# A fifth slot for expert weights in the memory of the modulation rows; modulation product on TensorE, state-space quarters begun among the projections

## What is computed

```
ada = silu(c) @ w_ada + b_ada
shift1, scale1, gate1, shift2, scale2, gate2 = split(ada, 6)
u = rms_norm(h, norm1_g) * (1 + scale1) + shift1
u_ssm, q, k, v, q_idx, k_idx, w_idx, g_ssm, g_attn = split(u @ w_in)
y_ssm = s5_mixer(u_ssm, ...)                     # diagonal complex scan, 32 groups x 64 states, GLU
y_attn = dsa_attention(q, k, v, q_idx, k_idx, w_idx)   # index scores, top-k keys, 8 heads, ALiBi
mixed = sigmoid(g_ssm) * (y_ssm @ w_proj_ssm) + sigmoid(g_attn) * (y_attn @ w_proj_attn)
h = h + gate1 * (mixed @ w_out)
u2 = rms_norm(h, norm2_g) * (1 + scale2) + shift2
h = h + gate2 * moe_ffn(u2)                      # sigmoid router, 64 experts of width 256, one shared
out = rms_norm(h, norm_f_g)
```

## Time and profile before

| | |
|---|---|
| Time, median of three runs | 1305.91 us (1305.76 to 1308.87) |
| Profiled execution | 1307.59 us, its span 1305.8 us |
| PE busy | 1139.6 us, 87% |
| DVE, ACT, POOL busy | 558.1, 221.6, 253.8 us |
| Issue to landing, median: w_ada piece, w_in item | 12.1 us, 9.1 us (2 MB each) |
| Issue to landing, median: expert gate, up, down | 11.8, 17.1, 17.5 us (1 MB each) |
| Bytes moved by DMA | 318.47 MB |

### The profile page before, as it was taken

One profiled execution on the slowest core, in us unless ns is written; L12 is line 12 of the kernel. 1 busy time (PEld: TensorE's weight loads), 2 busy tenths in 40 slices (PEclk: granted clock), 3 DMA queues, 4 the chain that ended last, 5 costly groups with the idle time before them and its releaser, 6 DMA issues. The chain is left out here.

```text
span 1305.8 us, 14750 instructions
## 1 busy us (share of the span) xinstructions
PE 1139.6 (87%) x5464; PEld 542.3 (42%) x5465; DVE 558.1 (43%) x1157; ACT 221.6 (17%) x440; POOL 253.8 (19%) x244
## 2 busy tenths in 40 slices
PE   0799677897999999998798999999999999998854
PEld 0544455644455444443433343444334344343222
DVE  5325989977745311334452222322222222222138
ACT  2411231104233200012001111111111111111101
POOL 7852477200000000002001111111111111111000
PEclk9799788898889999998998999999999999998977
DMA  8725100143131412120679999999999999999676
GB/s 326 187 94 180 55 10 10 42 161 129 35 159 64 162 64 81 65 88 18 241 290 348 422 404 416 417 408 419 416 389 416 398 421 387 403 399 396 245 323 265
DMA packets 84044, 318.47 MB, mean 244 GB/s; under 512 B 28978, under 2 KB 32050, under 8 KB 55298
## 3 DMA queue, kind: packets, MB, share of 16 engines
q1 hardware_dynamic: 64084, 277.96, 53.8%
q0 software_dynamic: 13488, 36.23, 7.2%
q10 hardware_dynamic: 6400, 3.33, 1.2%
HBM read 300.57 MB, written 28.31 MB: 252 GB/s over the span
## 5 line engine op out<-in xcount | busy, mean ns | idle before, releaser
L1526 PE MATMUL ps<-uTs,ring 128*128 128x512 f32 (+2 forms) x496 | 228.6, 619 | 3.4 <-DMA ring<-in_w_in 2.7
L1827 PE MATMUL ps<-ring,XT 128*32 128x512 f32 (+1 forms) x1472 | 216.7, 603 | 9.9 <-DMA ring<-in_w_exp_up 8.7
L1526 PEld LDWEIGHTS ps<-uTs,ring 128*128 128x128 f32 (+2 forms) x496 | 95.7, 197 | 123.0 <-issue 118.4
L1388 DVE TENSOR_TENSOR uTs<-uTs,ps 128x256 f32<-128x256 f32 x44 | 18.5, 421 | 281.3 <-ACT uTs L1007 281.3
L743 POOL DMA_INDIRECT XT<-u_rows,idx x45 | 45.9, 1020 | 400.9 <-DVE idx L1377 383.5
L1827 PEld LDWEIGHTS ps<-ring,XT 128*32 128x32 f32 (+1 forms) x1472 | 66.0, 120 | 137.9 <-issue 133.7
L1857 PE MATMUL ps<-ring,uTs 128*32 128x512 f32 (+1 forms) x736 | 112.5, 614 | 0.7 <-DMA ring<-in_w_exp_down 0.6
L1794 PE MATMUL ps<-ring,XT 128*128 128x512 f32 x224 | 98.4, 592 | 0.0
L1429 DVE TENSOR_SCALAR uTs<-ps,gat 128x512 f32<-128x512 f32 x44 | 33.1, 751 | 120.9 <-PE ps L1857 80.4
L596 POOL TENSOR_TENSOR ring<-ring 128x512 f32<-128x512 f32 (+4 forms) x35 | 56.8, 1622 | 79.3 <-issue 28.0
L1074 DVE SCALAR_TENSOR_TENSOR ADA<-ring,sm,ADA 128x2048 f32<-128x2048 f32 x24 | 60.2, 2507 | 27.5 <-DMA ring<-in_w_ada 13.9
(11 more groups left out here) (319 smaller groups left out, 1363.4 us busy)
## 6 DMA issues: line engine op xcount, KB each, us to landing
ring<-in_w_exp_gate SPq DMA_DIRECT2D x64, 1024.0 KB, 11.8
ring<-in_w_exp_up SPq DMA_DIRECT2D x64, 1024.0 KB, 17.1
ring<-in_w_exp_down SPq DMA_DIRECT2D x64, 1024.0 KB, 17.5
ring<-in_w_ada SPq DMA_DIRECT2D x12, 2048.0 KB, 12.1
ring<-in_w_in SPq DMA_DIRECT2D x7, 2048.0 KB, 9.1
ring<-expert_rows SPq DMA_DIRECT2D x6, 2048.0 KB, 18.4
ring<-in_w_out SPq DMA_DIRECT2D x2, 2048.0 KB, 8.7
H<-in_x SPq DMA_DIRECT2D x1, 2048.0 KB, 13.9
```

The costliest lines, as they stand in the source:

```text
L1526: ins = mm(b[0:rows_, 0:cols], l, r, start=(k == 0), stop=(k == len(chunks) - 1))
L1827: ins = mm(a3(ps[0][c, :], 2), xgT[par][:, k, c], wgu[r][:, k], start=(k == 0), stop=(k == KD - 1))
```

## The change

The products of silu(c) with w_ada move from DVE to PE. A piece is eight products: a column of silu(c) repeated 32 times as the stationary side, 512 weight columns moving, and four quarters of the 2048 columns in four 32-row parts of one PSUM bank, which is kept for it (`NB` falls from 6 to 5). DVE adds the bias once for each group of four pieces (`ada_row`), and `ada` picks a row with a column of the identity. The modulation rows no longer need 6144 columns of all partitions for long, so `ADA` becomes the fifth expert slot (`SLOTS`); the last modulation row moves to `GATE2`, the small table K16s into `ADA`. x is loaded first. The chunks of u are loaded before ("gs", 0). The first quarter's build and chunks are placed among the qi projections, its application before all index scores, and the build of the next quarter between gs and y. DVE's `top_k` of the second block moves into the first block's heads, that of the third into the second block's. POOL makes tables 2 and 3 earlier by a place.

```diff
-NB = 6
+NB = 5
 RING = 4
+SLOTS = RING + 1
...
+            sp.dma_start(H[:], a["x"][0].rearrange("(t p) d -> p t d", p=P)).then_inc(S["x_in"], 16)
...
             load(("A", 0))
-            sp.dma_start(H[:], a["x"][0].rearrange("(t p) d -> p t d", p=P)).then_inc(S["x_in"], 16)
             load(("A", 1))
...
             sp.dma_start(wg[3], weights("w_exp_gate", e3)).then_inc(gu_in[3], 16)
+            done(sp, ("gP", 0))
+            load_gate_up(4, e4)
+            load_down(4, e4)
             done(sp, ("dn", TT - 1, 1))
             sp.dma_start(wu[3], weights("w_exp_up", e3)).then_inc(gu_in[3], 16)
...
             s5_tables(1)
+            s5_tables(2)
             causal(1)
+            s5_tables(3)
             causal(2)
-            s5_tables(2)
             causal(3)
-            s5_tables(3)
...
+            def ada_row(part):
+
+                dve.wait_ge(b_in[part], 64)
+                dve.wait_ge(S["ada_sum"], 4 * (part + 1))
+                V.tensor_tensor(ada_rows[part], ada_rows[part], ps[5][:, :], ALU.add).then_inc(S["ada_row"], 1)
...
+            for q in range(NQ):
+                s5_scan(q)
+                if q + 1 < NQ:
+                    s5_phases(q + 1)
+                    s5_kernel(q + 1)
+                    index_scores(q + 1)
+            top_k(1, 0, 16)
+            ada_row(1)
...
-                    if n < TOPK // 8:
-                        top_k(3, n, n + 1)
+                    if i < 2:
+                        top_k(2 + i, 2 * h, 2 * h + 2)
...
+            def ada_piece(n):
+
+                part, j = n // 4, n % 4
+                w = a3(arrived(pe, ("A", n)), 2)
+                if n == 0:
+                    pe.wait_ge(S["c_silu"], 1)
+                elif j == 0:
+                    pe.wait_ge(S["ada_row"], part)
+                for k in range(2):
+                    col = csil[:, 2 * j + k:2 * j + k + 1].broadcast_to((P, 32))
+                    for q in range(4):
+                        ins = mm(ps[5][32 * q:32 * (q + 1), :], col, w[:, k, 512 * q:512 * (q + 1)],
+                                 start=(j == 0 and k == 0), stop=(j == 3 and k == 1))
+                ins.then_inc(S["ada_sum"], 1)
...
-            for c in range(2 * KD):
-                ins = mm(b[:, c:c + 1], ADA[:, P * c:P * (c + 1)], ones[:, 0:1], start=True, stop=True)
+            for c in range(4):
+                ins = tr(b[:, P * c:P * (c + 1)], ada_rows[0][:, P * c:P * (c + 1)])
...
+            ada_piece(4)
             s5_apply(0)
-            s5_build(1)
-            indexer(3)
-            s5_apply(1)
-            s5_build(2)
-            s5_apply(2)
-            s5_build(3)
-            s5_apply(3)
+            taken(pe, ("qiT", 3))
+            for q in range(1, NQ):
+                indexer(q)
+                s5_apply(q)
             w = a3(arrived(pe, ("q", 0)), 8)
             for m in range(4):
                 projection_t("qT", m, w, P * m)
+            ada_piece(7)
```

More of the change, by code:

```diff
@@ L504, in _ @@
                 load_down(n, e)
-            e2, e3 = expert_id(2), expert_id(3)
+            e2, e3, e4 = (expert_id(n) for n in range(2, 5))
             done(sp, ("out", TT - 1, 1))
@@ L538, in _ @@
                 with sp.If(n_ov > u):
-                    sp.wait_ge(S["expert_done"], LAST_PASS[NE - RING + u] + 1)
+                    sp.wait_ge(S["expert_done"], LAST_PASS[max(n for n in range(NE) if n % SLOTS == u)] + 1)
                     further(u, u)
@@ L1092, in rms_scale @@
                 link(V.tensor_tensor(rstd[:, c], rstd[:, c], newt[:, c], ALU.mult))
-            for n in range(2):
-                ada_piece(n)
             dve.wait_ge(S["squares"], 1)
@@ L1609, in _ @@
                 transposed_rows("uT", t, ut4)
[L1610 removed]
+            ada_piece(2)
+            ada_piece(3)
+            pe.wait_ge(S["ada_row"], 1)
             b = begin(("mod", 0))
[L1612 to L1613 removed]
+            for c in range(4):
+                ins = tr(b[:, P * c:P * (c + 1)], ada_rows[0][:, P * c:P * (c + 1)])
             end(ins)
[L1615 to L1616 removed]
             w = a3(arrived(pe, ("ssm", 0)), 8)
             for t in range(TT):
[L1619 removed]
+                b = begin(("ssm", t))
+                for k in range(KD):
+                    if t == 0:
+                        pe.wait_ge(S["u_ok_s" if k % 2 else "u_ok_v"], k // 2 + 1)
+                    ins = mm(b[:, :], uT[:, k, P * t:P * (t + 1)], w[:, k], start=(k == 0), stop=(k == KD - 1))
+                end(ins)
             pe.wait_ge(S["ct_in"], 256)
@@ L1633, in _ @@
             w = a3(arrived(pe, ("qi", 0)), 8)
-            for m in range(4):
+            for m in range(2):
                 projection_t("qiT", m, w, P * m)
-            taken(pe, ("qiT", 3))
+            s5_build(0)
+            projection_t("qiT", 2, w, P * 2)
+            chunks(0)
+            projection_t("qiT", 3, w, P * 3)
             def gates(name, half):
```

189 lines of the change are left out of this document (83 added, 106 removed).

## The result

The changed kernel takes 1298.1 us (median of 7 runs, 1295.9 to 1300.5); the kernel before, run beside it, 1310.3. The ratio is **0.9908**, with an interval of 0.9892 to 0.9925: 12 us faster, where 35 were forecast and the range ended at 1288. The forecast was counted from 1305.9; the ratio applied to that gives 1293.9, which is outside the range as well. The profiled execution has a span of 1296.5 us against 1305.8.

What follows compares the result with a forecast made beforehand. Three engines handing work over bound it to 293 us, PE to 640, full DMA engines with PE nearly full from 677. Terms -18 - 16 + 1.8 + 7.5 + 1 - 11 = -34.7 took 1305.9 to 1271 us; range 1256 to 1288.

Steps and rivals of the forecast that it cites:

- Start: Up to the ssm product: x loaded first and no accumulation on DVE, start at 35.5 us against 53.4, -18 us.
- Rival 4: The four 32-column products of a piece run one after another: 6.9 us instead of 1.8, total 1321 us; chance 0.04.
- the changes of tile shape: On PE: 24 changes cost 2.4 us at worst, taken as nothing; a drain of one record each would be 10 us.
- Quarters: Four state-space quarters: ends at 134, 168, 202 and 229 us against 262.8 for the last, -16 us beyond the start's gain.
- Elsewhere five are enough: Five accumulator banks instead of six suffice outside the glu and branch products, as each needed group was emptied earlier.
- First logits: Between the quarters and attention: the modulation piece behind q adds +1.8 us.
- Attention: Four blocks: -1.3 first, +5.3 second, +1.8 each third and fourth, sum +7.5; with about +1 behind it, +8.5.
- the +1.0 forecast: Behind attention, between glu and branch products: five accumulator banks and the bias row cost PE about +1 us.
- The +7.5: The sum of the four attention blocks in us, with bounds 0 and +13.
- Experts: Expert passes: the fifth slot fills the idle DMA gap, everything lands 7.6 us earlier, fewer waits for weights: -11 us.
- the five rivals: Slower tables 1283 (0.2), better slot and attention 1256 to 1264 (0.16), useless slot 1282 (0.09), serial tiles 1321 (0.04), unchanged (0.02).

Runs made afterwards that it cites:

- tables_later: Changed kernel with SyncE waiting for the modulation's fourth piece before issuing the state-space tables: ratio 0.99 to the kernel before.
- short_pieces: Changed kernel with the last four modulation pieces, inside attention, cut from 16 products of 32 columns to 4: ratio 0.9893 to the kernel before.
- no_w2: Changed kernel without GpSimd's second output table for the last three quarters: ratio 0.9855 to the kernel before.
- b_table_early: Changed kernel with GpSimd making the next quarter's input table right behind the current quarter's output table: ratio 0.9891 to the kernel before.
- topk_early: Changed kernel with top-k rounds placed as in the kernel before: ratio 0.9818, again 0.9831; 1287.5 us against 1296.9 for the changed kernel.
- four_slots: Changed kernel with four expert slots instead of five: ratio 0.9958 to the kernel before.
- light_down: Changed kernel loading only half of the down weights from the sixth expert on: ratio 0.9752 to the kernel before.
- topk_no_pieces: topk_early with every product of the last four modulation pieces cut from 512 to 32 columns: ratio 0.9806 to the kernel before.
- no_pieces: Changed kernel with every product of the last four modulation pieces cut from 512 to 32 columns: ratio 0.9863 to the kernel before.

## Why the prediction was wrong, point by point

No single term explains the miss; five of them missed by 1.3 to 7.7 us, all on the slow side. One step runs through three of them: PE's products were priced at full clock where they stand behind a wait.

- **Start, -18 against -14.6.** The mechanism and the small terms held: a piece takes 1.92 us (forecast 1.8), and the row, transposes and scaling took no longer than summed. The term that failed is the landing of the loads, "5.1 us a piece": the fourth piece came 2 us late and the ssm weights 3.4. The windows show 405 GB/s from 25.5 to 32.3 us, as assumed, but 285 from there to 38.8. tables_later excludes the small packets (291 GB/s there); why the last load is slow stays open.
- **Rival 4, tiles one after another.** It falls: 1.92 us, and short_pieces shows directly that one tile takes as long as four. The price of the changes of tile shape, taken as nothing, was not tested, as every kernel keeps them. In the rows nothing shows: the piece at 145.21 lasts 3.64 us (half clock), and the next product starts at 148.78.
- **Quarters, -16 against -9.** The chain that the prediction named, GpSimd's tables ahead of K, is there. From the end of y to the end of the tables it forecast 26.9 us; it was 25.0 and 26.8. What failed is the price of the products behind it, K 1.9 and y 5.3 at full clock, 7.2 together: they took 10.2 and 8.8. The K products made for the second, third and fourth quarter, then the last quarter's v1, v2 and gs products (2.0, 1.2 and 7.1 us at full clock):

```profile
128.97 1.92 PE L1566 MATMUL ps<-XT,ring 128*16 128x128 f32 x16
...
164.26 3.60 PE L1566 MATMUL ps<-ring 128*16 128x128 f32 x16 [4.02 <-POOL ring L694]
...
201.21 3.44 PE L1566 MATMUL ps<-XT,ring 128*16 128x128 f32 x16 [6.07 <-POOL XT L694]
...
220.36 3.65 PE L1584 MATMUL ps<-ring 128*128 128x64 f32 x16 [3.77 <-ACT ring L857]
223.94 1.98 PE L1590 MATMUL ps<-ring 128*64 128x64 f32 x32
225.84 8.31 PE L1513 MATMUL ps<-uTs,ring 128*128 128x512 f32 x16
```

  Of the 7 us, 1.9 lie before the first quarter's end (the ssm product took 30.3 us, priced at 27.7), 1.2 and 1.6 in the middle cycles (35.2 and 35.6 for 34) and 2.4 in the last (29.4 for 27), where GpSimd's last table also stretches the index multiplications; no_w2 takes 7 to 8 us of it away with that table. The sum also leaned on one engine alone: the same paragraph has DVE at 35 us, and b_table_early shows that taking GpSimd's waits away brings DVE's to the front. "Elsewhere five are enough" nearly held: 0.4 us of waiting for the K product's bank in the traced execution, 1.2 in others.
- **First logits, +1.8 against +3.1.** The piece came as priced; the q products took 29.3 us instead of 27.7.
- **Attention, +8.5 against +14.6.** The first block is +2.2 instead of -1.3. Its sum names no piece (1.9 us), and its second filler, behind a wait of 2.19 us, took 8.66 us instead of 7.04. The second block is +5.4, as forecast, but by luck: 22 + 7 + 1.8 + 3 is 33.8 us and not 35.6. The mechanism held there, with waits for exponentials of 6.2 us instead of 2.5. The third is +2.3 for +1.8; its half-clock spell was there before too. The fourth is +3.7 for +1.8: behind a wait of 1.78 us, the same in both kernels, its first filler took 8.36 us instead of 7.03. What follows gave the +1.0 forecast. The +7.5 also took the place of the top-k rounds as given; topk_early shows that this placement alone costs 10 us, about half of it clock.
- **Experts, -11 against some -3 in the pair of traces and -6.5 by four_slots.** The mechanism is right: the DMA engines set the waits of the passes (light_down), and the gap ahead of them is filled. The term is mis-sized: it took the gap (7.6) and added short gaps and clock, and the gap alone is as much as four_slots can show.
- Each of the five rivals changed one or two terms; none had all of them short at once. The range, from 1256 to 1288, was built the same way, so it could not hold a sum of five misses on one side.

## What to carry to other kernels

Price work that moves beside another engine by who holds what whole instructions at a time: halving the columns of VectorE's instructions saved little while GpSimd ran. Price the products behind a wait at the clock that rows behind such waits show, and not at that of the middle of a long run. Where two engines' sums come out at 34 and 35 us, removing one of them gains nothing; look for the third path too. And before a piece of work is held back behind a wait, look at how long its engine idles in that wait: one placement was worth 10 us, nearly as much as the whole change, though half of that hangs on a clock that came and went without a cause found here.

## What the runs showed of the hardware

- Seven scalar_tensor_tensor operations took 12.14 us at 256 columns and 11.61 at 128 beside GpSimd's table operations, 3.39 at 256 without them.
- A product on one column tile of 32 takes as long as four side by side: 1.90 and 1.92 us.
- After one and the same wait of 1.62 us the granted clock was 0.77, 0.50 and 0.71 in three stretches of 5 us in the changed kernel, 0.57 and 0.50 in topk_no_pieces, and 1.00 in topk_early and no_pieces. The block took 37.4 us in the changed kernel and 32.6 in topk_early.
